# Ten weight slots in place of nine, and expert weights cut by blocks of the contraction, in a two-layer model kernel

## The reference, cut to what is computed here

```python
affinity = softmax((h @ w_router), axis=-1)                      # 256 tokens x 16 experts
gate_vals, tok_idx = top_k(swapaxes(affinity, 1, 2), 32)         # 32 tokens for each expert
xs  = h[tok_idx]                                                 # 16 x 32 x 1024
hid = silu(xs @ w_gate[e]) * (xs @ w_up[e])                      # 1024 -> 1024 each
ye  = (hid @ w_down[e]) * gate_vals                              # 1024 -> 1024
y   = zeros(256, 1024).at[tok_idx].add(ye)
```

## Time and profile before

| | us |
|---|---|
| median of three runs | 1847.29 (1846.15 to 1850.33) |
| the profiled execution | 1843.14 |
| its span on the core | 1841.1 |
| mean granted TensorE clock, as a share of 2.4 GHz | 0.943 |
| PE busy | 1612.3 (88% of the span) |
| DVE busy | 725.6 (39%) |
| ACT busy | 372.2 (20%) |

### The profile page before, as it was taken

How to read it: one execution, slowest core, us unless ns; L and a number is a source line. 1 busy time by engine, 2 the same in 40 slices (tenths; PEclk the granted TensorE clock), 3 DMA queues, 4 the chain that set the end, 5 groups by cost and what they waited for, 6 DMA issues and landing times.

```text
span 1841.1 us, 29008 instructions
## 1 busy us (share of the span) xinstructions
PE 1612.3 (88%) x12716; PEld 1070.1 (58%) x12716; DVE 725.6 (39%) x1325; ACT 372.2 (20%) x871; POOL 77.2 (4%) x94
## 2 busy tenths in 40 slices
PE   9999998989998757575564899999999999999998
PEld 5675557858845213121211376769984677589963
DVE  1005475676554000000000235556664255646663
ACT  2110133444422101010000224320000225210000
POOL 0000003304120000000000000000000000000000
PEclk9999999989999878787877999999999999999999
DMA  8621120040177999999999842224454532125550
GB/s 367 259 91 47 30 90 2 4 183 3 32 310 290 430 431 431 430 431 430 431 430 430 322 187 92 78 105 179 149 223 182 207 127 78 60 114 207 184 194 23
DMA packets 35584, 381.90 MB, mean 207 GB/s; under 512 B 6978, under 2 KB 10434, under 8 KB 12674
## 3 DMA queue, kind: packets, MB, share of 16 engines
q1 hardware_dynamic: 35458, 380.04, 51.1%
HBM read 378.98 MB, written 1.05 MB: 206 GB/s over the span
## 4 chain that ended last, share of the span: by engine, by line
PE 51%; DMA 12%; DVE 3%; ACT 2%; issue 1%; DVEq 0%
PE psum L2945 15%; DMA weight_ring<-in_w_moe 8%; PE psum L2000 8%; PE psum L3007 7%; PE psum L2326 6%; DMA arena<-in_w_moe 4%; PE psum L2329 3%; PE psum L1973 3%; PE psum L2479 2%; PE psum L2467 1%; PE psum L162 1%; PE psum L2446 1%; PE psum L2355 0%; PE psum L2432 0%; PE psum L1955 0%
## 5 line engine op out<-in xcount | busy, mean ns | idle before, releaser
L2000 PE MATMUL psum<-weight_ring,arena 128*32 128x512 f32 x624 | 143.3, 728 | 103.2 <-DMA weight_ring<-in_w_moe 51.6
L2945 PE MATMUL psum<-arena 128*128 128x128 f32 x1408 | 165.2, 275 | 1.7 <-DVE arena L3143 1.7
L2945 PEld LDWEIGHTS psum<-arena 128*128 128x128 f32 x1408 | 161.1, 192 | 2.0 <-issue 2.0
L2146 DVE COPY arena<-psum 128x512 f32<-128x512 f32 x16 | 11.1, 691 | 351.3 <-PE psum L2000 351.3
L2000 PEld LDWEIGHTS psum<-weight_ring,arena 128*32 128x32 f32 x624 | 36.9, 131 | 174.4 <-issue 174.4
L2945 PE MATMUL psum<-arena,weight_ring 128*128 128x128 f32 x1056 | 127.9, 277 | 6.3 <-DVE arena L3181 4.2
L2945 PEld LDWEIGHTS psum<-arena,weight_ring 128*128 128x128 f32 x1056 | 123.3, 194 | 8.6 <-issue 5.8
L2000 PE MATMUL psum<-arena 128*32 128x512 f32 x400 | 88.8, 716 | 44.5 <-DMA weight_ring<-in_w_moe 44.5
L2326 PE MATMUL psum<-arena,weight_ring 128*128 128x256 f32 x512 | 118.5, 382 | 0.3 <-ACT arena L2541 0.3
L1371 PE MATMUL psum<-arena 64*64 64x64 f32 x3328 | 109.1, 223 | 10.9 <-POOL arena L1542 8.2
L1371 PEld LDWEIGHTS psum<-arena 64*64 64x64 f32 x3328 | 101.7, 137 | 17.2 <-POOL arena L1542 8.6
(11 more groups left out here) (497 smaller groups left out, 2292.1 us busy)
## 6 DMA issues: line engine op xcount, KB each, us to landing
weight_ring<-in_w_moe SPq DMA_DIRECT2D x55, 2048.0 KB, 22.3
arena<-in_w_moe SPq DMA_DIRECT2D x41, 2048.0 KB, 24.8
weight_ring<-in_w_in SPq DMA_DIRECT2D x23, 2048.0 KB, 9.9
weight_ring<-in_w_mod SPq DMA_DIRECT2D x12, 2048.0 KB, 12.1
weight_ring<-in_w_gate SPq DMA_DIRECT2D x12, 2048.0 KB, 7.9
weight_ring<-in_w_up SPq DMA_DIRECT2D x12, 2048.0 KB, 7.8
weight_ring<-in_w_down SPq DMA_DIRECT2D x12, 2048.0 KB, 7.8
weight_ring<-in_w_out SPq DMA_DIRECT2D x6, 2048.0 KB, 8.4
```

The costliest lines, as they stand in the source:

```text
L2000: last = nc.tensor.matmul(K.ps[strip(j), 4, :], xsT[:, e // 4 % 2, k, strip(e % 4)], ws[j][:, k, :], start=(k == 0), stop=(k == KT - 1), s ...
L2945: last = nc.tensor.matmul(K.ps[:, bank, P * n:P * n + P], lhs, rhs, start=(n == 0 and k == 0 and name in ("m1", "m5", "m6")), stop=(k == 3 ...
```

## The change

- The expert weights are laid out by blocks of the contraction. A gate-up transfer s holds blocks 2s and 2s+1 for all 2048 columns, a down transfer i the four contraction blocks of hidden strip half i for all 1024 columns. Size and number of transfers stay the same.
- The gate-up product takes one transfer, does its 8 products, gives the slot back with the last of them and takes the next. The fourth slot comes back with the first transpose. The down product goes the same way in two steps of 8 products.
- The scatter of the expert before now stands ahead of the gate-up product.
- In the last expert two unit products stand before the gate-up product, after each of its first three transfers and after the first down transfer, ten in all.
- In the last expert ACT copies only the first half of the down result, and DVE copies the second; the last scatter waits for both.

```diff
-NX = 4
+NX = 5
@@ outputs, sync
-                W.load_early(sp, W.first_expert + NB)
+                for n in range(NX - 3):
+                    W.load_early(sp, W.first_expert + NB + n)
@@ route_and_experts, tensor
         def scatter(e):
             pe.wait_ge(parts_kept, e + 1)
+            if e == NE - 1:
+                pe.wait_ge(half_kept, 1)
...
         for e in range(NE):
-            ws = [W.take(pe) for _ in range(4)]
+            if e:
+                scatter(e - 1)
+            if e == NE - 1:
+                keep_busy(nc, K, 7, 2)
...
-            for k in range(KT):
-                for j in range(4):
-                    last = nc.tensor.matmul(K.ps[strip(j), 4, :], xsT[:, e // 4 % 2, k, strip(e % 4)],
-                                            ws[j][:, k, :], start=(k == 0), stop=(k == KT - 1),
-                                            skip_group_check=True)
+            for s in range(4):
+                w = W.take(pe).rearrange("p (k j) n -> p k j n", j=4)
+                for i in range(2):
+                    k = 2 * s + i
+                    for j in range(4):
+                        last = nc.tensor.matmul(K.ps[strip(j), 4, :], xsT[:, e // 4 % 2, k, strip(e % 4)],
+                                                w[:, i, j, :], start=(k == 0), stop=(k == KT - 1),
+                                                skip_group_check=True)
+                if s < 3:
+                    last.then_inc(W.used, 1)
+                    if e == NE - 1:
+                        keep_busy(nc, K, 7, 2)
             last.then_inc(gu_made, 1)
-            if e == 0:
-                pe.wait_ge(gu_made, 1)
-                nc.tensor.nop().then_inc(W.used, 4)
-            if e:
-                scatter(e - 1)
...
-                if e and c == 0:
-                    last.then_inc(W.used, 4)
+                if c == 0:
+                    last.then_inc(W.used, 1)
...
-            wd = [W.take(pe) for _ in range(2)]
...
-            for n in range(2):
-                for i in range(2):
+            for i in range(2):
+                w = W.take(pe).rearrange("p (j n) d -> p j n d", n=2)
+                for n in range(2):
                     for j in range(4):
...
+                if i == 0:
+                    last.then_inc(W.used, 1)
+                    if e == NE - 1:
+                        keep_busy(nc, K, 5, 2)
             last.then_inc(down_made, 1)
             pe.wait_ge(down_made, e + 1)
-            nc.tensor.nop().then_inc(W.used, 2)
+            nc.tensor.nop().then_inc(W.used, 1)
@@ scalar
-            for n in range(2):
+            for n in range(2 if e < NE - 1 else 1):
@@ vector
+        dve.wait_ge(down_made, NE)
+        dve.wait_ge(y_made, NE - 1)
+        nc.vector.tensor_copy(parts[:, 1, :], K.ps[:, 7, :]).then_inc(half_kept, 1)
@@ layout
-    a["w_moe"] = np.concatenate([np.stack([slots(w[e]) for e in range(NE)]) for w in (wg, wu, wd)], 1).reshape(6 * NE, P, -1)
+    gu = np.concatenate([wg, wu], 2).reshape(NE, 4, 2, P, 4, 512).transpose(0, 1, 3, 2, 4, 5).reshape(NE, 4, P, SLOT)
+    down = wd.reshape(NE, 2, 4, P, 2, 512).transpose(0, 1, 3, 2, 4, 5).reshape(NE, 2, P, SLOT)
+    a["w_moe"] = np.concatenate([gu, down], 1).reshape(6 * NE, P, SLOT)
```

More of the change, by code:

```diff
@@ L1934, in route_and_experts @@
     down_made, parts_kept, y_made, y_squared = K.sem("down_made"), K.sem("parts_kept"), K.sem("y_made"), K.sem("y_squared")
-    ones_sqrt = K.sem("ones_sqrt")
+    ones_sqrt, half_kept = K.sem("ones_sqrt"), K.sem("half_kept")
     ms_ready, rooted, x_ready = K.sem("ms_ready"), K.sem("rooted"), K.sem("x_ready")
@@ L2029, in tensor @@
                 pe.wait_ge(wide_kept, 2 * ahead + 2)
-            for n in range(2):
-                for i in range(2):
+            for i in range(2):
+                w = W.take(pe).rearrange("p (j n) d -> p j n d", n=2)
+                for n in range(2):
                     for j in range(4):
-                        k = 2 * j + i
-                        last = nc.tensor.matmul(K.ps[strip(j), 6 + n, :], hidT[:, k // 4, k % 4, :],
-                                                wd[n][:, k, :], start=(i == 0), stop=(i == 1),
+                        last = nc.tensor.matmul(K.ps[strip(j), 6 + n, :], hidT[:, i, j, :],
+                                                w[:, j, n, :], start=(i == 0), stop=(i == 1),
                                                 skip_group_check=True)
+                if i == 0:
+                    last.then_inc(W.used, 1)
+                    if e == NE - 1:
+                        keep_busy(nc, K, 5, 2)
             last.then_inc(down_made, 1)
             pe.wait_ge(down_made, e + 1)
-            nc.tensor.nop().then_inc(W.used, 2)
+            nc.tensor.nop().then_inc(W.used, 1)
             if e == 0:
@@ L3288, in first_and_second_block @@
     K.nc, K.dram, K.out = nc, dram, out
-    K.A = Arena(nc, 127 * 256 + 4 * KT)
+    K.A = Arena(nc, 127 * 256 + 4 * KT + SLOT)
     K.W = WeightStream(nc, dram)
@@ L3477 @@
     from concourse.bass_utils import run_bass_kernel_spmd
-    nc = bacc.Bacc("TRN2", target_bir_lowering=False, num_devices=1)
+    nc = bacc.Bacc("TRN2", target_bir_lowering=False, num_devices=1, dynamic_dma_scratch_size=512)
     arrays, dram = {}, {}
```

## The result

| | kernel before | changed kernel |
|---|---|---|
| median, us | 1846.72 (1844.84 to 1850.33, 4 runs) | 1830.9 (1828.99 to 1836.64, 4 runs) |
| the profiled execution, us | 1843.14 | 1836.64 |
| its span, us | 1841.1 | 1834.6 |

A forecast was written before the change was run, and what follows sets the result against it. The prediction took the expert stage to be bound by full-rate weight transfers plus the work after the last landing. Gains of 4.9 + 2.5 + 7.7 = 15.1 us took 1847.3 to 1832.2 us, range 1828 to 1840.5.

The forecast's parts named there:

- What bounds the stage: Expert stage: a stream of weight transfers at full DMA rate, 4.88 us each, plus work after the last landing.
- The stream: Last expert landing comes earlier: 4.9 us from one transfer fewer, 2.5 us from the first slot coming back sooner.
- no other loss would follow: After the first expert, DMA engines never run dry, although gate-up of expert 1 starts some 4.6 us later.
- The work behind T: From the last expert transfer's landing (T) to the last scatter's start: 2.9 us in place of 10.6, 7.7 less.
- PE is free at T - 1.0: Last expert: PE finishes half of down and two unit products 1.0 us before the last expert transfer lands.
- within two blocks: Gate-up behind the moved scatter starts 1.7 us late and catches up, at 1.8 us of work in 4.88.
- Rival A: Last expert: PE late or at the low clock, costing 2 to 4 us; 1835.2 us with 3; chance 0.23.
- The clock: Last expert's tail: low clock could cost up to 4 us, taken as 0, against the skill's advice on short pieces.
- B: Expert stage: the stream does not end earlier, only the tail's 7.7 us is gained; 1839.6 us; chance 0.10.
- C: Expert stage: PE at 1.2 GHz becomes the bound, 49 us slower over 14 experts; 1881 us; chance 0.03.
- The sum: Whole kernel: 4.9 + 2.5 + 7.7 = 15.1 us less, giving a median of 1832.2 us.
- The parts at nothing: The early transfer ahead of the expert stage and the moved scatter were put at no cost.

The follow-up runs named there:

- e2: Changed kernel with nine slots instead of ten, arena and scratch as before; ratio to the kernel before 0.9932.
- e4: Changed kernel with slots given back together, four with the first transpose and two after down; ratio to the kernel before 0.9948.
- e1: Kernel before plus only the tenth slot, its larger arena, smaller scratch and the extra early transfer; ratio to the kernel before 0.9964.
- e9: Changed kernel with one unit product instead of two in each of the five places of the last expert; ratio to the kernel before 0.9928.
- e7: Changed kernel with ACT copying both halves of the last down result; no ratio, 449.3 us from first expert-stage transfer issue to unit products behind the last scatter.
- e8: Changed kernel profiled and timed again without an edit; ratio to the kernel before 0.9923.
- e10: Changed kernel, second early transfer issued 27 us later; no ratio, 449.4 us from first expert-stage transfer issue to unit products behind the last scatter.
- e3: Changed kernel without the ten unit products of the last expert; ratio to the kernel before 0.9925.
- e6: Changed kernel with each gate-up product waiting for all four transfers before it starts; ratio to the kernel before 0.9985.
- e5: Changed kernel with the scatter of the expert before put back behind the gate-up product; ratio to the kernel before 0.9928.
- e11: Changed kernel with one unit product per place and two ring transfers issued earlier, in stage outputs; median 1826.8 us, ratio to the kernel before 0.9883.

## Why the prediction was right, point by point

**What bounds the stage.** Right. Between 600 and 1000 us the engines move 431 GB/s on the average in the changed kernel too, a transfer takes 4.88 us (29.3 us for the last six), and what comes behind the stage is as long as before (803.1 and 802.8 us).

**The stream: 4.9 + 2.5 = 7.4 us.** T - S is 7.3 us shorter. The terms apart, by taking each away from the changed kernel: nine slots give 447.1, 5.0 us more (e2); slots given back together 446.0, 3.9 us more (e4). Alone, the slot gave 4.1 us (e1), the blocks 2.3 (e2). Most of what is missing between 4.1 and 5.0 is that the first gate-up product of e1 starts 0.7 us later after S; and of the 3.9 of e4, 1.2 are the later return that its edit makes. So the terms add up to within half a microsecond. That no other loss would follow, although gate-up of expert 1 starts later, held: cut into stretches of 8 us from 584 to 1024 us, the stage table shows no less than 424 GB/s in any.

**The work behind T: 7.7 us.** It was 6.4 in the changed kernel's profile. The mechanism held, T + 2.9 occurs exactly (e2, e4, e9). The step that was mis-sized is "PE is free at T - 1.0". I took the clock at entry as full and gave a pair of unit products 1.7 us; between blocks a pair takes 1.91. And the sentence that a late start would be caught up "within two blocks" counted 1.8 us of work in 4.88, without the pairs: in the last expert work and pair are 3.8 us. Even from full clock all four gate-up blocks then run without a wait (e7: at 995.86, 999.62, 1003.39 and 1007.16 us, a pair between them), and PE is just in time at the end. Such a margin is used up by any fall of the clock. Rival A named the rest: down and scatter of expert 14 partly at the lower clock, 2.86 + 5.51 in place of 1.9 + 3.7, and units that keep PE late. It asked 2 to 4 us for it; it cost 1.3. So the profiled execution, and e8, are forecast and rival A in one; in e10 it is A's other half, a fall inside the last expert, for 0.6. With hindsight 0.23 looks too little a chance: three of the six executions with two units and the scatter ahead show one or the other (the changed kernel, e8 and e10, but not e2, e4 and e7). Its price was too high.

**The clock.** The rule of the Trainium skill ("TensorE: Matmul & The Clock Gate", section HAM oscillation), not to cut the work into pieces between waits, was the argument against the change. Its mechanism is in the runs: without units the last half of down and the scatter run at 1.2 GHz (e3). But its advice, the whole contraction behind one wait, doesn't pay here. In e6 it loses 12.5 us of distance, with 8.9 us of unit products on the path; what is left is that the long wait lets the clock fall too, and that the work comes behind the last landing. The measurement decides for the pieces. Whether one unit product between them is better than two is seen in the distances only.

**Rivals B and C.** Not seen. B would have left T - S at 449; C is excluded by PE's waits for transfers, and by a granted clock of 0.86 and 33.5 of 50 us busy in the middle of the stage.

**The sum and the runs.** From S to the end the changed kernel is 13.7 + 0.3 = 14.0 us shorter, the ratio says 12 to 19. I had taken the stages ahead of S as fixed. They are not: S moves by 7.7 us between executions even without e11, whose edit lies ahead of it, and the two profiled executions compared here happen to stand 7.6 us apart in it. Comparing their spans alone would have given 6.5 us. That the forecast lies within 1.3 us of the median has some luck in it. The tail gave 1.3 us less than the sum had, so the traces show 14.0 of the 15.1 us, and the interval of the runs, 12 to 19 us, can't tell 14.0 from 15.1.

**The parts at nothing.** The moved scatter (e5) was free as it ran, and gained nothing against an entry at the low clock, but 1.0 us against one at full clock. DVE's copy is worth its 0.3 us (e7). The early transfer was put at nothing; that isn't shown. Up to 1 us in the landing that line 183 waits for, and with it 1 to 4 us from the start of that line's products to S in some executions, stay open (e10).

## What to carry to other kernels

Where weights stream at the full rate, two things count: how much is in flight before the first slot comes back, and how little work stands behind the last landing. Cut the contraction so that each landing has its own piece of work and its own slot to give back; it pays at both ends of the stream and nowhere between. Products that only hold the clock must be fewer than the wait that they fill: count work and filler for each landing against the time between landings, with the engine entering late and slow, and leave a margin.

## What the runs showed of the hardware

- The wake of PE from a landing is 0.04 us where it waits for one transfer, against 0.24 us in the kernel before, where it waits for four and then for a count of DVE's copies that had long been reached, and 0.14 us in e6, where the four waits come last. What makes the difference wasn't tried.
- A pair of unit products takes 1.72 us behind the scatter, but 1.91 us behind gate-up or down blocks, which fill the array by strips. The 0.2 us were in none of the rows above of the kernel before.
- With pieces of 1.9 us in 4.9 the clock doesn't settle at either level. In e9 the last four pieces of expert 14 took 1.92, 3.54, 1.92 and 1.92 us, and the last two of expert 15 3.53 and 1.92; the mean over 50 us was 0.86 in the changed kernel.
- The start of the expert stage varied between 574.2 and 581.9 us over thirteen executions whose work ahead of it is the same but for one early transfer (e11, which changes more there, came to 584.8); that is half of what the whole change is worth. The start of line 183's products, which comes before that transfer, already varied between 504.9 and 510.1 us in them.
